# The first attention's lag: logits ahead of the split's low part, copies ahead of exponentials, and block-key scores that share their banks

## What is computed

```
q, k, v, ... = split(rmsnorm(x) @ w_in)
block keys/values: mlp over windows of 32 tokens, stride 16 (15 of them)
p_cmp  = softmax(q @ k_cmp.T / 8 + bias_cmp)      # 8 heads per group, 2 groups
p      = softmax(q @ k.T / 8 + bias)              # 16 heads x 2 branches, 16 SWA heads
o      = gate0 * (p_cmp @ v_cmp) + gate1 * o_1 + gate2 * o_2, and o_swa
x      = x + concat(o, o_swa) @ w_out
```

## Time and profile before

| | |
|---|---|
| median of 3 runs | 3240.4 us (3237.48 to 3242.87) |
| profiled execution | 3230.95 us |
| its span | 3229.2 us |
| PE, DVE, ACT busy | 97%, 60%, 46% of the span |
| mean granted clock of PE | 0.984 |
| woven attention | from 142.6 us to about 337 us |
| PE busy in it | 126.55 of 141.40 us (142.6 to 284), 17.49 of 20.00 (284 to 304), 27.16 of 33.00 (304 to 337) |

### The profile page before, as it was taken

How to read it: one execution, slowest core, us unless ns; L and a number is a source line. 1 busy time by engine, 2 the same in 40 slices (tenths; PEclk the granted TensorE clock), 3 DMA queues, 4 the chain that set the end, 5 groups by cost and what they waited for, 6 DMA issues and landing times.

```text
span 3229.2 us, 52467 instructions
## 1 busy us (share of the span) xinstructions
PE 3130.6 (97%) x20546; PEld 2874.7 (89%) x20546; DVE 1935.3 (60%) x2575; ACT 1489.6 (46%) x1977; POOL 13.9 (0%) x27
## 2 busy tenths in 40 slices
PE   7998989999999999999999999999999999998999
PEld 7987889999999999988888888898789999998887
DVE  4356567964666665455555555766566666666444
ACT  3244443444555554444444444534455555554333
POOL 1000000000000000000000000000000000000000
PEclk9899999999999999999999999989999999999999
DMA  7322434655556566666666666444445554554554
GB/s 255 108 82 100 162 132 162 203 196 200 190 215 218 197 226 244 226 241 240 243 235 245 239 244 243 155 142 144 157 170 182 183 182 182 182 182 165 182 193 175
DMA packets 132893, 615.15 MB, mean 190 GB/s; under 512 B 12158, under 2 KB 49231, under 8 KB 66993
## 3 DMA queue, kind: packets, MB, share of 16 engines
q1 hardware_dynamic: 126176, 583.05, 51.3%
q10 hardware_dynamic: 5296, 21.93, 2.2%
q0 software_dynamic: 1328, 8.89, 0.7%
HBM read 578.13 MB, written 36.49 MB: 190 GB/s over the span
## 4 chain that ended last, share of the span: by engine, by line
PE 88%; DVE 6%; ACT 3%; issue 2%; DMA 2%; ACTq 0%; DVEq 0%; SPq 0%
PE bank L588 86%; DMA raw<-in_experts_u_t 1%; DVE low L1162 1%; ACT high L2030 1%; ACT big L2100 1%; PE bank L678 0%; DVE big L1272 0%; ACT big L2107 0%; DVE big L1281 0%; DVE big L1540 0%; DVE big L1545 0%; DVE big L1543 0%; DMA resid<-in_x 0%; DVE big L1497 0%; DVE big L1283 0%
## 5 line engine op out<-in xcount | busy, mean ns | idle before, releaser
L1162 DVE TENSOR_TENSOR low<-raw,high 128x1024 fp32r<-128x1024 f32 x1008 | 1227.6, 1224 | 1171.8 <-ACT high L2030 1167.9
L2030 ACT ACTIVATE high<-raw 128x1024 fp32r<-128x1024 f32 x1008 | 1060.1, 1058 | 1316.1 <-PE bank L588 1096.5
L588 PE MATMUL bank<-act_high,high 128*128 128x256 f32 x4240 | 1219.3, 288 | 26.6 <-DVE low L1162 13.5
L588 PE MATMUL bank<-act_low,high 128*128 128x256 f32 x4240 | 1206.7, 285 | 0.0
L588 PE MATMUL bank<-act_high,low 128*128 128x256 f32 x4240 | 1206.5, 285 | 0.0
L588 PEld LDWEIGHTS bank<-act_high,high 128*128 128x128 f32 x4240 | 821.2, 194 | 31.9 <-DVE low L1162 15.0
L588 PEld LDWEIGHTS bank<-act_low,high 128*128 128x128 f32 x4240 | 821.6, 194 | 1.0 <-issue 1.0
L588 PEld LDWEIGHTS bank<-act_high,low 128*128 128x128 f32 x4240 | 820.7, 194 | 0.0
L588 PE MATMUL bank<-high,weighed_high 128*128 128x512 f32 x1024 | 398.4, 389 | 2.1 <-DVE weighed_low L1595 2.1
L588 PE MATMUL bank<-low,weighed_high 128*128 128x512 f32 x1024 | 398.3, 389 | 0.0
L588 PE MATMUL bank<-high,weighed_low 128*128 128x512 f32 x1024 | 398.3, 389 | 0.0
(11 more groups left out here) (267 smaller groups left out, 2244.2 us busy)
## 6 DMA issues: line engine op xcount, KB each, us to landing
raw<-in_experts_u_t SPq DMA_DIRECT2D x128, 1024.0 KB, 5.2
raw<-in_experts_v_t SPq DMA_DIRECT2D x128, 1024.0 KB, 4.8
raw<-in_w_up_t SPq DMA_DIRECT2D x88, 1024.0 KB, 4.8
raw<-in_w_in_t SPq DMA_DIRECT2D x68, 1024.0 KB, 4.8
raw<-in_w_down_t SPq DMA_DIRECT2D x44, 1024.0 KB, 4.8
raw<-in_w_out_t SPq DMA_DIRECT2D x32, 1024.0 KB, 4.8
raw<-in_peer_wq_t SPq DMA_DIRECT2D x16, 1024.0 KB, 4.8
hidden_dram<-big SPq DMA_DIRECT2D x64, 256.0 KB, 5.4
```

The costliest lines, as they stand in the source:

```text
L588: return pe.matmul(out_, lhs_t, rhs, start=start, stop=stop, skip_group_check=True)
L1162: dve.tensor_tensor(low[b][:, :], raw[r][:, HALF * which:HALF * (which + 1)], as_f32(high[b][:, :]), ALU.subtract).then_inc(low_ready[b], 1)
L2030: act.activation(high[b][:, :], raw[r][:, HALF * which:HALF * (which + 1)], ACT.Copy).then_inc(high_ready[b], 1)
```

## The change

It has four parts. DVE handles slot 2p ahead of `split_low` of half p+3 in the projection's loop (in the output product nothing is moved). ACT copies a pair's transposes two slots behind its scores and ahead of the exponentials of the pair in that slot, instead of three slots behind and after them. The block-key scores of one tile of tokens go into columns 384 to 511 of banks 2 and 3, between the two parts of the scores at slot 16, and those of the other at slot 18; DVE reads them just ahead of that pair's logits, as 8 operations of 64 elements instead of 4 of 128. The transposes of the block-key probabilities go into the spare columns of banks 4 and 5 behind the pairs' transposes at slots 31 and 33, two each, and ACT copies them with those (`cmp_copied`) instead of DVE. Sets then have all turns of banks 6 and 7 to themselves up to the block-key mixes.

```diff
-                turn=2 * double + g + (double > 1) + (double > 3) + (4 if double > 4 else 0), at=DH * j))
-        CMP_SCORES_TURN, CMP_PROBS_TURN, CMP_MIX_TURN = 4, 9, 12
+                turn=2 * double + g + (4 if double > 4 else 0), at=DH * j))
+        CMP_MIX_TURN = 10
+        CMP_SCORES_WITH = {NSA_UNITS // 2 + 2 * i: i for i in range(TT)}
+        CMP_PROBS_WITH = {NSA_UNITS - 4 + 2 * g: g for g in range(2)}
...
                     for u in units1[n:n + 2]:
                         m = mm(bank[:, 2 + u["g"], at:at + keys], u["q"][:, tokens], u["k"][:, 0:keys])
+                    if n in CMP_SCORES_WITH and at == 0:
+                        cmp_scores(CMP_SCORES_WITH[n])
...
+                if n in CMP_PROBS_WITH:
+                    pe.wait_ge(cmp_dve, 7)
+                    for i in range(TT):
+                        m = pe.transpose(bank[:, 4 + i, 3 * P:N], cmp_logits[:, CMP_PROBS_WITH[n], i, :, :].rearrange("p h c -> p (h c)"),
+                                         ident[:, :])
...
-                if slot == 19:
-                    cmp_scores()
-                elif slot == 35:
-                    cmp_turn()
-                elif 43 <= slot < 47:
+                if 43 <= slot < 47:
                     cmp_mix(slot - 43)
...
+            def cmp_scores(i):
+
+                for h in range(GROUP_HEADS):
+                    at = 3 * P + CMP_COLUMNS * (h % SET)
+                    mm(bank[:, 2 + h // SET, at:at + CMP_COLUMNS], q1[:, h, P * i:P * i + P],
+                       cmp_k[:, :, :].rearrange("p g c -> p (g c)"))
...
             def cmp_mix(n):
 
+                pe.wait_ge(cmp_copied, n // 2 + 1)
                 pe.wait_ge(set_read, CMP_MIX_TURN + n - 1)
...
+                if n in CMP_SCORES_WITH:
+                    cmp_logits_part(CMP_SCORES_WITH[n])
                 dve.scalar_tensor_tensor(at[:, :, 0:T], scores_[:, :, 0:T], DH ** -0.5, bias[:, :, 0:T], ALU.mult, ALU.add)
...
+            def cmp_logits_part(i):
+
+                for g in range(2):
+                    for n in range(2):
+                        heads = slice(SET * n, SET * n + SET)
+                        note(dve.scalar_tensor_tensor(
+                            cmp_logits[:, g, i, heads, :],
+                            bank[:, 2 + n, 3 * P:N].rearrange("p (h g c) -> p h g c", g=2, c=CMP_PAD)[:, :, g, :],
+                            DH ** -0.5, cbias[:, i, GROUP_HEADS * g + SET * n:GROUP_HEADS * g + SET * n + SET, :], ALU.mult, ALU.add))
...
-                elif slot == 35:
-                    dve.wait_ge(cmp_pe, 5)
-                    settle()
-                    dve.tensor_copy(cmp_probs_t.rearrange("p n q -> p (n q)"), bank[:, 6 + CMP_PROBS_TURN % 2, :]).then_inc(set_read, 1)
...
                 for p in range(QUAD):
+                    attention_slot(KT * (g - 3) + 2 * p)
                     split_low(half("w_in_t", p + LOOKAHEAD, g))
-                    attention_slot(KT * (g - 3) + 2 * p)
...
                 act.wait_ge(probs_turned, n + 2)
                 act.wait_ge(mixed, n)
+                if n in CMP_PROBS_WITH:
+                    g = CMP_PROBS_WITH[n]
+                    act.activation(cmp_probs_t[:, 2 * g:2 * g + 2, :], bank[:, 4:6, 3 * P:N], ACT.Copy).then_inc(cmp_copied, 1)
                 act.activation(probs_t1[:, :, :], bank[:, 4:6, 0:3 * P], ACT.Copy).then_inc(probs_copied, 2)
...
+                if slot - 2 in pair_at:
+                    copy_probs1(pair_at[slot - 2])
                 if slot in pair_at:
                     exps1(pair_at[slot])
...
-                if slot - 3 in pair_at:
-                    copy_probs1(pair_at[slot - 3])
```

More of the change, by code:

```diff
@@ L57 @@
 CMP_PAD = 16
+CMP_COLUMNS = 2 * CMP_PAD
 BUCKETS, EXACT, MAX_DIST = 32, 16, 2048
@@ L348, in build @@
         cmp_act = sem("cmp_act")
+        cmp_copied = sem("cmp_copied")
         cmp_shifted = sem("cmp_shifted")
@@ L837, in attention_slot @@
                     attention_mix(pair_at[slot - 4])
-                if slot == 19:
-                    cmp_scores()
-                elif slot == 35:
-                    cmp_turn()
-                elif 43 <= slot < 47:
-                    cmp_mix(slot - 43)
[L845 to L863, removed]
+                if 43 <= slot < 47:
+                    cmp_mix(slot - 43)
+            def cmp_scores(i):
[3 more added lines that the diff above has]
+                       cmp_k[:, :, :].rearrange("p g c -> p (g c)"))
             def cmp_mix(n):
+                pe.wait_ge(cmp_copied, n // 2 + 1)
                 pe.wait_ge(set_read, CMP_MIX_TURN + n - 1)
@@ L899, in turn_o1 @@
                     if n == 0 and half_:
-                        pe.wait_ge(set_read, UNITS // SET + 6)
+                        pe.wait_ge(set_read, UNITS // SET + 4)
                     elif n == 0:
@@ L1318, in cmp_set @@
                 at = 16 * g + 8 * i
-                dve.wait_ge(cmp_pe, 6 + n)
+                dve.wait_ge(cmp_pe, 4 + n)
                 dve.tensor_tensor(share1.rearrange("p (h d) -> p h d", d=DH), bank[:, 6 + (CMP_MIX_TURN + n) % 2, :].rearrange("p (h d) -> p h d", d=DH),
@@ L1324, in cmp_set @@
                 add_o1(part_, share1)
-            def cmp_logits_done():
[L1328 to L1337, removed]
+            def cmp_logits_part(i):
[6 more added lines that the diff above has]
+                            DH ** -0.5, cbias[:, i, GROUP_HEADS * g + SET * n:GROUP_HEADS * g + SET * n + SET, :], ALU.mult, ALU.add))
+            def cmp_logits_done():
+                settle()
                 link(dve.tensor_reduce(cmp_stat[:, 0, :], rows_c, AX.X, ALU.max))
```

## The result

The changed kernel takes 3214.3 us (median of 4, 3209.8 to 3216.9) against 3239.8 for the kernel before beside it: a ratio of 0.9919, 95% interval 0.9902 to 0.9936. Timed again in another group of runs it was 0.9934 (0.9913 to 0.9956), 3210.1 against 3232.8. So it is faster by 0.7 to 0.8%, 21 to 26 us; forecast were 17.7 us and 3222.7. The kernel before had medians of 3239.8, 3236.0 and 3232.8 us in the three groups of runs (this one, experiments 1 to 4, experiments 5 to 8), so times are compared within a group only. The direction and the mechanism hold; the size was short by a sixth to a third, and the time lies 0.3 us inside the lower edge of the range, which is luck as much as reckoning.

A forecast was written before the change was run, and what follows sets the result against it. PE bounds the kernel, delayed in the woven attention by a DVE-ACT ring of 6.85 us a pair against its 5.91. Terms -10.5 - 1.4 - 1.7 + 0.5 - 6.0 + 1.4 = -17.7 us gave 3222.7 us, range 3214 to 3232.

The forecast's parts named there:

- the term of the clock: Woven attention: three low-clock stretches follow waits that go, -6.0 us; one new stretch behind the narrow block, +1.4 us.
- query copies: DVE's query copies that PE waits for, 5.0 us in all: left unchanged, 0, bounds -1.0 and +2.3 us.
- The ring: DVE and ACT waiting for each other, 6.85 us a pair; would close over two pairs, leaving PE's 5.91 us as pace.
- Waits for the copy: Woven attention: all 9 PE waits for ACT's copy of the turned probabilities go, -10.5 us.
- Set reads: Block-key scores and transposes no longer wait for DVE's set reads, -1.4 and -1.7 us; next wait at slot 20, +0.5.
- Block-key work: Block-key matmuls at the same price, DVE's smaller operations and ACT's copies hidden: 0 us.
- Start of the output product: Slots 48 to 56: exponentials of pair 42 start 1.8 us later behind the copy, but covered: 0 us.
- The difference carries over: Whole kernel: the first profile's 9.45 us below the median was added to the profiled forecast of 3213, giving 3222.7 us.
- A: Woven attention: the copy stays late because its transposes come late on PE; -2.4 us, or 3238 us; chance 0.06.
- B: After the stage: something not on PE takes the gain back, 3240 us, or 3232 in part; chance 0.08.
- C: Projection's loop: narrow matmuls leave PE at 1.2 GHz behind every pair; +13 us, or 3253 us; chance 0.06.
- D: Woven attention: no new low stretch, no set wait, query copies 1 us cheaper; -20.6 us, or 3220 us; chance 0.15.

The follow-up runs named there:

- experiments 1 to 4: Second group of runs: DVE's order alone, ACT's order alone, block-key banks alone, the kernel before unchanged; median of the kernel before 3236.0 us.
- experiments 5 to 8: Third group: both orders without banks, the changed kernel again, more of DVE's order, block-key scores in four pairs; median of the kernel before 3232.8 us.
- experiment 1: Kernel before with only DVE's order changed (slot 2p ahead of `split_low` in the projection's loop): ratio 0.9947 (0.9928 to 0.9965).
- 5: Kernel before with both orders changed (DVE's and ACT's), block-key work as before: ratio 0.9943 (0.9921 to 0.9965).
- 2: Kernel before with only ACT's order changed (copy two slots behind the scores, ahead of the exponentials): ratio 0.9990 (0.9977 to 1.0003).
- Experiment 3: Kernel before with only the block-key scores and transposes moved to spare columns of banks 2 to 5: ratio 0.9993 (0.9980 to 1.0007).
- experiment 8: Changed kernel with the 16 block-key score matmuls spread over four pairs instead of two: ratio 0.9941 (0.9918 to 0.9964) to the kernel before.
- 7: Changed kernel with query copies ahead of a group's last `split_low`, and slots ahead of it in the output product: ratio 0.9949 to the kernel before.

## Why the prediction was right in kind and short in size

The step that failed is the term of the clock, put at -4.6 us and measured at -8.6; beside it the query copies, put at 0, gave -1.9, and the first profile was taken to lie as far below the median after the change as before it.

- *The ring.* Right. Scores are 5.91 us apart, and the copy is waited for by nobody. That the ring now closes over two pairs is reckoned, not seen: it paces nobody any more. But its two halves aren't equal: DVE's order opens the ring (experiment 1), ACT's adds the slack for the last 2 us (5), and alone gives nothing (2). The text ahead treated them as one edit.
- *Waits for the copy, -10.5.* Measured 10.2 to 12.4 in four profiles of before, 0 in three of after.
- *Set reads, -3.1, and +0.5 next.* Right. At slot 20 the second set's read ended at 209.82, and the scores stood at 208.03 and 214.27, 6.24 apart, so 0.3 us (0.3 and 0 in the two other profiles). Experiment 3 shows what the arithmetic hides: with the ring closed these 3.1 us are no gain.
- *Query copies, 0 (bounds -1.0 and +2.3).* -1.9, outside. PE's wait behind group 3 was 0.94 and behind group 4 0.73, where it had been 1.75 twice. My own numbers (DVE free at 3.5 us, PE there at 3.5, two copies 1.3) gave 1.3 each, and I left 1.75 standing. In the trace DVE was free 3.3 us after the scores and PE came at 3.6.
- *Block-key work, 0.* Nearly. DVE's four operations of 64 elements took 0.62, twice 0.6 as taken. The 8 matmuls cost PE 2.1 us (8.01 less 5.91) in place of 1.88, half of 3.76: 0.4 in all. So two scores stood 8 us apart at the full clock, which by the text ahead would have meant the clock: as a sign it was wrong.
- *Start of the output product, 0.* Right: no wait for the copy or for scores there.
- *The clock, -6.0 + 1.4 = -4.6.* **This is the term that failed in size**: it measured -8.6, counted over all profiles. In the first pair it was -6.8, of which the projection's loop alone, which the term was about, gave -5.1. So the execution that I had read was reckoned nearly right; it was the others that weren't like it. The new low stretch behind the narrow block came where it was put (194.4 to 197.8). The Trainium skill ("TensorE: Matmul & The Clock Gate", "What's actually happening") tells the clock by how busy PE has been; by that rule, as I read it, there would have been none there. The traces decide against that reading. What was missing: the execution I had read had 13.6 us at the lower clock in the projection's loop; the four have 13.6 to 27.2, 18.7 in the mean, against 4.6 after. That is 7 us of the term, and most of the difference from what I had read is the stretch behind the block-key scores, three times as long in two profiles. The rest, 1.3 us, lies at the start of the output product, which I left as it was (two stretches at 308 and 315 us before, one at 297 after, in the first pair). The low time there differs by 10 us between two executions of the changed kernel, so that part may be chance. "All three follow waits that go" was also too simple: the waits of the copy went, and their two stretches with them, but the one behind the narrow block stayed in experiments 1 and 5, 13.7 and 10.3 us long, though the wait ahead of the block was smaller (0.79 in place of 1.45).
- *From one profile to the median.* "The difference carries over" was the second fault. The first execution lay 9.4 us below the median. About 4 of it was its tail, chance; the rest is of the size by which the stage varies with the clock (208 to 217 us), and that is a loss that the change reduces. That this rest is the stage's clock is argued, since the executions of the median have no profile. As far as it is, it doesn't carry over, and it should have widened the range downwards.

The sum for the first pair of profiles closes: copy -10.5, sets -3.1, query copies -1.9, the wait for `act_low` +1.2 (2.44 to 3.63; 2.2 to 3.6 in the four profiles of before, so chance), 13.6 us less at half clock -6.8: -21.1, against -20.9 measured. The rivals: A, B and C did not happen; D lay nearest and had the query copies right, but its main reason (no new stretch) was not.

How much of the 21 to 26 us lies in the clock outside the stage, what makes one execution's low stretches longer than another's, and whether the banks and experiment 8 are worth their 1 to 5 us of stage in the times, stays open: the intervals are 5 to 8 us wide either way.

## What to carry to other kernels

When two engines idle in turn for each other, write the ring down, and ask of each edit over how many steps the ring closes afterwards: moving the one instruction that closes it (here `split_low`) gave most of the gain, shortening it by a link gave none, and removing waits of another kind was taken back by it. Where PE idles for a microsecond or two between bursts, or does a few microseconds of narrow matmuls, the price can be the wait and a low clock behind it. The second doesn't follow every wait: of the seven waits over 1.2 us ahead of 300 us in the first profile, three had a low stretch behind them. It also varies from one execution to the next; take more than one profile before sizing it.

## What the runs showed of the hardware

The kernel before has the same waits in four executions to within about 3 us (23.1 to 26.2), but 20 to 34 us at 1.2 GHz in the stage.

The narrow matmuls and the clock can be followed through all thirteen profiles. Seven have one block of 16 block-key score matmuls (32 columns, 32 records, about 4 us back to back): the four of before and experiments 1, 2 and 5. In each a stretch of 3.4 to 13.7 us at the lower clock begins within that block. Five have two blocks of scores, 8 such matmuls and a mix (64 columns), about 4 us each: the three of the changed kernel and experiments 3 and 7. Each of them has 3.5 to 6.9 us at the lower clock, beginning at the end of one of the blocks or of both. Experiment 8 has 4 such matmuls in each of four blocks, and its one profile shows no low stretch there. It has the same wait of 0.94 us ahead of the first block as the changed kernel, so that wait alone doesn't make the difference; one profile is thin evidence all the same.
